# Recurrence gates of a hybrid encoder layer: one mixed contraction tile for both neighbours, put together by DMAs inside SBUF

## What is computed

```python
D_RNN = 1280; N_LRU_BLOCKS = 16; LRU_BLOCK = 80; LRU_C = 8.0
def rg_lru_branch(u, conv_w, conv_b, w_rg, b_rg, w_ig, b_ig, lru_lambda):
    u = depthwise causal convolution of width 4 over u, + conv_b
    ub = u.reshape(B, S, N_LRU_BLOCKS, LRU_BLOCK)
    r = sigmoid(einsum("bsnc,ncd->bsnd", ub, w_rg) + b_rg)
    i = sigmoid(einsum("bsnc,ncd->bsnd", ub, w_ig) + b_ig)
    log_a = -LRU_C * r * softplus(-lru_lambda)
    a = exp(log_a)
    b = sqrt(-expm1(2.0 * log_a)) * (i * u)
    _, h = lax.associative_scan(_lru_combine, (a, b), axis=1)   # h = a * h_before + b
    return h
...
h = rms_norm(x); proj = h @ w_in      # -> lru_u, lru_y, q, k, v, two merge gates
lru_out = rg_lru_branch(lru_u, ...) * gelu(lru_y)
attn_out = sliding window attention with sinks (q, k, v)
merged = g_lru * (lru_out @ w_lru_br) + g_attn * (attn_out @ w_attn_br)
x = x + rms_norm(merged @ w_out);  x = x + rms_norm(SwiGLU(rms_norm(x)))
```

## Time and profile before

| | us |
|---|---|
| median of three runs | 1734.54 |
| profiled execution, its own time | 1732.49 |
| its span | 1730.7 |
| PE busy / DVE / ACT / POOL | 1692.4 / 801.4 / 561.0 / 1320.2 |
| mean granted TensorE clock | 0.991 |
| gate matmuls (L424 to L426 on uc_hi, uc_lo) | 3 x 108 |

### The profile page before, as it was taken

The page is one execution under the profiler, slowest core; times in us unless marked ns, Lnnn a source line. Parts: engine busy times, 40 slices in busy tenths (PEclk is TensorE's granted clock), DMA queues, the critical chain, the costliest instruction groups (busy, mean ns, idle before and its releaser), DMA issues.

```text
span 1730.7 us, 26755 instructions
## 1 busy us (share of the span) xinstructions
PE 1692.4 (98%) x7676; PEld 1392.5 (80%) x7676; DVE 801.4 (46%) x878; ACT 561.0 (32%) x1034; POOL 1320.2 (76%) x1344
## 2 busy tenths in 40 slices
PE   8999999999999999999999999999999999999995
PEld 6787888888888878888888888888888888888884
DVE  5899736651277987766421733211611232111013
ACT  4577435442236765254422322111200211111000
POOL 5799966777788999777777877776777777666774
PEclk8999999999999999999999999999999999999997
DMA  4333332232343333422323434322433343224331
GB/s 142 102 88 89 116 98 85 79 98 94 108 128 106 90 89 108 155 75 76 96 94 103 140 130 143 109 96 93 137 100 95 111 143 132 94 95 141 96 97 60
DMA packets 111228, 183.15 MB, mean 106 GB/s; under 512 B 12352, under 2 KB 38208, under 8 KB 111168
## 3 DMA queue, kind: packets, MB, share of 16 engines
q1 hardware_dynamic: 97056, 156.15, 29.2%
q10 hardware_dynamic: 14112, 26.22, 4.5%
HBM read 173.94 MB, written 8.39 MB: 105 GB/s over the span
## 4 chain that ended last, share of the span: by engine, by line
PE 86%; issue 5%; POOL 4%; DVE 3%; ACT 1%; DMA 0%; POOLq 0%; ACTq 0%; SPq 0%; DVEq 0%
PE ps L426 27%; PE ps L425 26%; PE ps L424 26%; POOL w_hi L358 3%; POOL w_lo L361 1%; PE ps L486 1%; PE ps L565 1%; PE ps L487 1%; PE ps L488 1%; PE ps L555 0%; PE ps L557 0%; PE ps L556 0%; PE ps L580 0%; PE ps L579 0%; DVE rows L1482 0%
## 5 line engine op out<-in xcount | busy, mean ns | idle before, releaser
L361 POOL TENSOR_TENSOR w_lo<-w_raw,w_hi 128x512 fp32r<-128x512 f32 (+2 forms) x664 | 849.4, 1279 | 55.4
L358 POOL TENSOR_SCALAR w_hi<-w_raw 128x512 fp32r<-128x512 f32 (+2 forms) x664 | 466.5, 703 | 334.2 <-PE ps L426 261.1
L424 PE MATMUL ps<-h_hi,w_hi 128*128 128x512 f32 x1376 | 538.1, 391 | 9.9 <-POOL w_lo L361 7.5
L426 PE MATMUL ps<-h_hi,w_lo 128*128 128x512 f32 x1376 | 541.0, 393 | 0.0
L425 PE MATMUL ps<-h_lo,w_hi 128*128 128x512 f32 x1376 | 538.8, 392 | 0.0
L424 PEld LDWEIGHTS ps<-h_hi,w_hi 128*128 128x128 f32 x1376 | 258.4, 188 | 71.2 <-issue 6.4
L425 PEld LDWEIGHTS ps<-h_lo,w_hi 128*128 128x128 f32 x1376 | 258.4, 188 | 57.3
L426 PEld LDWEIGHTS ps<-h_hi,w_lo 128*128 128x128 f32 x1376 | 258.6, 188 | 54.3
L1122 DVE TENSOR_TENSOR acc<-acc,sq 128x512 f32<-128x512 f32 x55 | 66.3, 1206 | 226.7 <-ACT sq L969 201.7
L1447 DVE TENSOR_TENSOR tmp<-ps,tmp 128x512 f32<-128x512 f32 x44 | 30.4, 691 | 301.8 <-PE ps L426 301.8
L426 PE MATMUL ps<-f_hi,w_lo 128*128 128x512 f32 x352 | 138.7, 394 | 0.0
(11 more groups left out here) (193 smaller groups left out, 2431.3 us busy)
## 6 DMA issues: line engine op xcount, KB each, us to landing
w_raw<-w_f SPq DMA_DIRECT2D x176, 256.0 KB, 3.0
w_raw<-w_step SPq DMA_DIRECT2D x64, 256.0 KB, 2.6
w_raw<-w_b SPq DMA_DIRECT2D x64, 256.0 KB, 3.0
w_raw<-w_d SPq DMA_DIRECT2D x64, 256.0 KB, 2.7
w_raw<-w_a SPq DMA_DIRECT2D x96, 128.0 KB, 2.0
xs<-x_t ACTq DMA_DIRECT2D x32, 256.0 KB, 3.4
w_raw<-w_q SPq DMA_DIRECT2D x32, 256.0 KB, 3.2
w_raw<-w_o SPq DMA_DIRECT2D x32, 256.0 KB, 3.0
```

The costliest lines, as they stand in the source:

```text
L358: nc.gpsimd.tensor_scalar(w_hi[:, s, w], w_raw[:, s, w], 1.0, 0.0, ALU.mult, ALU.add).then_inc(w_hi_made, 1)
L361: nc.gpsimd.tensor_tensor(w_lo[:, s, w], w_raw[:, s, w], rd(w_hi[:, s, w]), ALU.subtract).then_inc(w_lo_made, 1)
L424: mm(out, w_hi[:, s, w], x_hi, start=(k == 0), stop=False)
L426: last = mm(out, w_lo[:, s, w], x_hi, start=False, stop=(k == total - 1))
```

## The change

For the six tiles with two neighbours (`MIXED` = 1, 2, 3, 6, 7, 8), the rows of the neighbours on which the gates depend lie in the upper half of tile j-1 (partitions 64 to 127) and in the lower half of tile j+1 (partitions 0 to 63). The change gathers these two halves in one tile, `mix_hi` and `mix_lo`, three buffers of each, in the memory of `v_hl`. ACT issues the gathering: in a new function `mix(h, j)`, called between `decay` and `gelu`, it copies partitions 0 to 63 of tile j into the mixed tile for j-1, and partitions 64 to 127 into the one for j+1, each as two DMAs (hi and lo). So tiles 2 and 7 issue four DMAs, the other tiles two each: 24 in each half. PE waits for the mixed tile's semaphore (all four DMAs) ahead of the gates of a mixed tile, and every gate has then 2 contraction tiles (tile 5 leaves out its zero one): 20 a gate, 40 in each half.

SP loads the weights of the gates in the same form: for a mixed block two DMAs of 64 partitions bring the neighbours' weight rows into one tile, a third brings the tile's own. POOL splits 256 columns in place of 384 and waits for two semaphores. In both streams the step and tail parts are written out in place of the loop. The weights in DRAM are unchanged.

```diff
+MIXED = (1, 2, 3, 6, 7, 8)
+GATED = {"step": 0, "tail": 8}
...
+        mix_hi = at("mix_hi", [P, 3, T], F32R, reg_v + 4 * KV_HEADS * 2 * HD)
+        mix_lo = at("mix_lo", [P, 3, T], F32R, reg_v + 4 * (KV_HEADS * 2 * HD + 3 * T))
...
+            def load_gates(dram, g, sizes, n, i0):
...
+                    wait_pos(sp_eng, w_lo_made, n + b - RING + 1)
...
+                    elif i in MIXED:
+                        sp_eng.dma_start(w_raw[0:P // 2, s, P:2 * P],
+                                         dram[g, 0:P // 2, off + 2 * P:off + 3 * P]).then_inc(mix_loaded[s], 16)
+                        sp_eng.dma_start(w_raw[P // 2:P, s, P:2 * P],
+                                         dram[g, P // 2:P, off:off + P]).then_inc(mix_loaded[s], 16)
+                        sp_eng.dma_start(w_raw[:, s, 0:P], dram[g, :, off + P:off + 2 * P])\
+                            .then_inc(w_loaded[s], 16)
...
+            def split_gates(sizes, n, i0):
...
+                    s, w = b % RING, slice(0, (4 if size == 4 else 2) * P)
...
+                        pool.wait_ge(mix_loaded[s], 32 * used[s])
...
+            def gates(h, j, n, slot):
+                J = j + KR * h
+                pe.wait_ge(uc_lo_made, J + (1 if j == KR - 1 else 2))
...
+                if j in MIXED:
+                    pe.wait_ge(mix_made[j % 3], 64 * (2 * h + 1 + (j > 5)))
+                tiles = [(j + d) % 4 for d in ((0, 1) if j in (0, 5) else (-1, 0))]
                 for g in range(2):
-                    project(4 + g, n + g, slot + g, [size], uc_hi, uc_lo, tiles=tiles)
+                    s, out = (slot + g) % RING, ps[:, 4 + g, :]
+                    pe.wait_ge(w_lo_made, n + g + 1)
+                    for k in range(2):
...
+                        mm(out, w_hi[:, s, w], x_hi, start=(k == 0), stop=False)
+                        mm(out, w_hi[:, s, w], x_lo, start=False, stop=False)
+                        last = mm(out, w_lo[:, s, w], x_hi, start=False, stop=(k == 1))
...
+            def mix(h, j):
+                if j + 1 in MIXED or j - 1 in MIXED:
+                    act.wait_ge(uc_lo_made, j + KR * h + 1)
+                for to, r in ((j - 1, slice(0, P // 2)), (j + 1, slice(P // 2, P))):
+                    if to in MIXED:
+                        act.dma_start(rd(mix_hi[r, to % 3, :]), rd(uc_hi[r, j % 4, :])).then_inc(mix_made[to % 3], 16)
+                        act.dma_start(rd(mix_lo[r, to % 3, :]), rd(uc_lo[r, j % 4, :])).then_inc(mix_made[to % 3], 16)
...
                     gate_root(h, j - 2)
                     decay(h, j - 2)
+                    mix(h, j)
                     gelu(h, j, n + 6, j % 4)
```

More of the change, by code:

```diff
@@ L214, in build @@
         w_loaded = [sem(f"w_loaded{i}") for i in range(RING)]
+        mix_loaded = [sem(f"mix_loaded{i}") for i in range(RING)]
+        mix_made = [sem(f"mix_made{i}") for i in range(3)]
         par_loaded = sem("par_loaded")
@@ L316, in load @@
                     off += size * P
+            def load_gates(dram, g, sizes, n, i0):
+                off, i, half = 0, i0, slice(0, P // 2)
+                for b, size in enumerate(sizes):
+                    s = b % RING
+                    wait_pos(sp_eng, w_lo_made, n + b - RING + 1)
+                    if size == 4:
+                        sp_eng.dma_start(w_raw[:, s, 0:CAP], dram[g, :, off:off + CAP])\
+                            .then_inc(w_loaded[s], 16)
[5 more added lines that the diff above has]
+                        sp_eng.dma_start(w_raw[:, s, 0:P], dram[g, :, off + P:off + 2 * P])\
+                            .then_inc(w_loaded[s], 16)
+                    else:
+                        at0 = off + (size - 2) * P
+                        sp_eng.dma_start(w_raw[:, s, 0:2 * P], dram[g, :, at0:at0 + 2 * P])\
+                            .then_inc(w_loaded[s], 16)
+                    off += size * P
+                    i += size < 4 and sizes[b - 1] < 4
             def stream(stages, bases):
@@ L323, in stream @@
                     first = 1 if base == 0 else 0
+                    if name in GATED:
+                        for g in range(groups):
+                            load_gates(dram, g, sizes, base + g * len(sizes), GATED[name] + 4 * g)
+                        continue
                     if first:
@@ L369, in stream @@
                     first = 1 if base == 0 else 0
+                    if name in GATED:
+                        for g in range(groups):
+                            split_gates(sizes, base + g * len(sizes), GATED[name] + 4 * g)
+                        continue
                     assert base % RING == 0 and len(sizes2) % RING == 0
@@ L500, in recurrent @@
                     project(0, n, slot, UNIT, h_hi, h_lo)
[L501 to L505, removed]
+                    gates(h, j - 2, n + 2, slot + 2)
                     wait_pos(pe, gelu_made, j + KR * h)
```

32 lines of the change are left out of this document (25 added, 7 removed).

## The result

The changed kernel takes 1739.07 us (median of ten runs, 1736.87 to 1742.36), the kernel before 1734.45 us in ten runs on the same chip (1731.69 to 1736.47). The ratio is 1.003, 95% interval 1.002 to 1.004: 0.3% slower, where 0.1% faster had been forecast. The time lies inside the predicted range, on the wrong side of the forecast.

The account below looks back on a forecast made before the run. It took the ACT loop, with gates waiting for copies behind decay, to set the pace: +1.85 us first half, -3.4 second, -1.6 in sum, 1734.54 to 1732.9 us. Range 1726.5 to 1740.

Parts of the forecast that it names:

- POOL's term: Gate blocks of 256 instead of 384 columns save POOL 0.76 us a step, 4.6 us a half over six steps.
- the loop on ACT: Step from gates through tanh, exp, root, DVE and decay back to gates; D(0) to D(7) forecast at 101.8 us.
- POOL as the bound: Rival: POOL stays the bound, mixed wait hidden, late start made up; 4.6 us a half, 1725.4 us, chance 0.13.
- The mixed step: Steps whose gates wait for copies issued behind decay: 5.5 us to the tanh plus 9.1 to decay, 14.6 us.
- The issue: Copies on ACT's queue behind D(i-1): 0.05 us to the first issue, 0.35 to the second, an issue taking 0.33.
- The landing: Copies inside SBUF: 2.0 us to land, as stores on the same queue, range 1.6 to 3.0.
- From tanh to decay: Part of a mixed step from the gate's tanh to its decay: 9.1 us, with POOL having less to do.
- The unmixed step: Two of seven steps (gates 4 and 5) have no mixed tile and keep the loop at 14.4 us.
- the clock falls more often: Rival: half clock also in the second half's G(1) or in G(6); 2.7 or 5.4 us, 1735.6 to 1738.3, chance 0.14.
- the late landing: Rival: copies land at 3.0 us, mixed steps take 15.2; 4.0 us a half, 8.0 in all, 1740.9, chance 0.18.
- The head: Tile 1's copies ahead of its gelu on ACT make D(0) 1.55 us late in each half, bounds 0.7 and 2.
- What was put at nothing: Steps' issues under decay (upper bound 0.3 us a step), SP's extra issues and the written-out streams (0 to 2 us): 0.

Follow-up runs that it names:

- nothing is paid: Changed kernel without copies; mixed gates contract over the left neighbour's tile, output not the reference's: 1720.71 us, ratio 0.9926 to the kernel before.
- where no gate waits: Changed kernel, copies issued but gates of a mixed tile not waiting for them: 1729.11 us; with the head's copies also moved behind the gelu: 1725.33 us.
- the early copies: Changed kernel with the steps' copies issued between root and decay instead of behind decay, head's copies unmoved: 1720.91 us, ratio 0.9929 to the kernel before.
- filling: Changed kernel with 6 to 16 unused matmuls on PE ahead of the wait before G(1), G(3) and G(6): 1735.30 us, ratio 1.0012 to the kernel before.
- POOL alone: Changed kernel without copies, POOL splitting 256 columns but PE still doing three contraction tiles: 1723.79 us, ratio 0.9947 to the kernel before.

## Why the prediction was wrong, step by step

**What bounds the kernel.** That PE's 86% of the chain would not turn into 19.2 us was right: 12.8 us come when nothing is paid. The forecast worked out POOL's term but did not put it in the sum, which went by the loop on ACT; POOL as the bound was a rival. With no copy in the way POOL is the higher limit (15.88 us a step with 384 columns, 14.95 with 256, against PE's 15.1 with 66 matmuls), and its 0.76 us a step was sized right. The sum also took it that what moves the tanh of gate 8 moves the end; from there to Q(2) the change saves 1.1 and 1.25 us, which it had left out.

**The mixed step.** The mechanism was right: gates behind the copies, copies behind decay, tanh behind the gates, and the stage's end with the tanh of gate 8. What failed is the price of the wait: 5.5 us from D(i-1) to the tanh of gate i, the same for every mixed gate. The trace has 6.1 at its best (87.17 to 93.31 for D(1) and gate 2), 6.7 and 6.8 for gate 8, and 7.5 to 9.9 for gates 1, 3 and 6. With all that follows from it the wait costs 9.5 us of the kernel. The terms:

- *The issue.* 0.05 and 0.35 with 0.33 an issue, from the loads of the earlier trace rows. Measured 0.47 and 0.61: the lo copy leaves at +0.51 and its issue ends at +1.12.
- *The landing.* 2.0 with a range of 1.6 to 3.0, its lower end from a saving by half the bytes for which no row was given. Measured 2.3 for hi and 2.8 for lo in the median, never under 2.2, and up to 4.6, above the range. By the Trainium skill (DMA: Bandwidth & Descriptors, Anatomy of one DMA), whose fit for DMAs issued by GpSimd has a term for the bytes as well, 128 KB would be an estimated 2.3 us. These copies are issued by ACT. The row of hi agrees with the estimate all the same; the lo copy right behind it does not. The prediction had named only the fixed part and left open that an SBUF target would answer sooner, which these rows don't show.
- *From tanh to decay* 9.1 were put down; it is 8.2 (78.95 to 87.17) and 8.4 (93.31 to 101.68). This was too high by about as much as the other two were too low in an undisturbed step. So the 14.6 of a mixed step was met (14.51) by two errors that cancel, which is luck. The unmixed step of 14.4 came as forecast (14.26 and 14.51).

**The steps that were not ordinary.** Between D(0) and D(7) the trace has 107.7 us in the first half and 110.8 in the second, where 104.5 (with one fall of the clock) and 101.8 were forecast; before it was 103.4 and 106.0. All of the miss between these two decays lies in six steps: those behind G(1), G(3) and G(6). There the gates start 3.9 to 5.2 us after decay, or the clock is at half, or both. The forecast had one fall of the clock, in G(1) of the first half, which came, with the start at 73.35 in place of 71.9; it made G(1) 2.3 us longer, where 2.7 were put down. It came four more times: G(6) in the first half and G(1), G(3) and G(6) in the second. That was the rival called "the clock falls more often", with a chance of 0.14 and a price of 2.7 or 5.4 us, 1735.6 to 1738.3. The other rival that points this way is the late landing, 1740.9. The measured 1739.1 lies between them, and both came together, which no case of the prediction allowed for, since each was worked out with the other at its likeliest value. The landing rival's own slope, 8 us for 1 us of landing, gives 1739.3 with the median of 2.8; that is chance, since it made every mixed step longer by 0.6, while the undisturbed ones stayed at 14.51 and the loss sat in three gates a half and in ACT's issues.

**The head.** 1.55 us a half were put down. The gelu of tile 1 starts 3.15 us later than in the earlier trace rows (46.43 to 49.58). Of this 1.1 lie ahead of the first copy: the stage starts that much later in this trace (`uc_hi` of tile 0 at 36.41, before at 35.30). The other 2.0 are the copies of tile 1. So D(0), 2.2 us later than in the earlier trace rows, is 1.1 us later by the head in the first half, less than put down, and in the second half 1.6 (28.29 against 26.73 us from `uc_hi` of tile 0), as put down. Against the same kernel with the head's copies moved it is 1.2 and 2.8, so something else in the change gives 1.2 back in the second half. The runs that load and split as the change does and have no copies ahead of the head's gelu take 25.5 us there, the one that only leaves matmuls out on PE 26.7. By the ratios the head's copies cost 4.9 us in both halves, or 3.3 where no gate waits, and 3.1 were in the sum: within what the ratios leave open, the term was right.

**What was put at nothing.** The copies' issues in the steps were called free under decay, "upper bound 0.3 us a step". They are not free: 5.2 us in sixteen steps, 0.3 a step, the upper bound. Two issues hold ACT by 0.52 us ahead of the gelu, four by 1.85. Part of it is seen in the step of tile 7; how the rest reaches the end was not followed further. SP's two more issues a block show no wait of POOL for a gate's load in the trace of the changed kernel. What the written-out streams cost was not measured apart; it lies within the 12.8 us.

**The signs in the profile.** Right: 84 matmuls less, POOL below 95%, half clock in G(1), the gates behind decay, steps of 14.4 to 14.7 where nothing disturbs (14.3 to 14.5). Wrong: 2.5 us from decay to gates (3.0 to 5.2), and the tanh of gate 8 (184.64 and 668.66, not 179.4 and 652.5). The gelu of tile 1 (49.58, not 48.0) and `conv_in` of tile 2 (60.23, not 59.5) came late, mostly with the start of the stage.

**The account by ratios.** 12.8 us gained by fewer tiles; 8.5 lost by issuing the copies where they stand (3.3 head, 5.2 steps); 9.5 lost by waiting for them, some 3.1 or more of it by the clock. That is +5.2 in sum, 0.3%. These differences add up by their making; what confirms them are the two kernels that undo a cause alone in the changed kernel: the head moved gives 4.9 back, and the early copies give 17.5 of the 18.0, though the head's copies stand where they stood. The prediction's -1.6 us had the loss at one wait of 5.5 us a step and one fall of the clock, and the issues in the steps at nothing; these are the steps of it that failed.

**Still open.** Why some landings take over 4 us where most take 2.3 to 2.8: no run was made for it. In the 3 us behind decay the DMA engines of the changed kernel are busy for 0.73 to 0.79 ahead of the late G(3) and G(6) of both halves, with SP's weight loads issued up to and across the copies, and for 0.58 to 0.62 ahead of G(2) and G(7), which start after 3.0 us. So loads at the same time are a likely cause, not a shown one, and G(8), after 3.5 and 3.7 us with the engines at 0.54, does not fit. How much of the wait is the clock: filling gave back 3.1 us, with two falls left, and in the one trace five pairs of gates were 9.1 to 9.5 us longer; nothing here narrows it further.

## What to carry to other kernels

Issue a DMA that feeds the next matmuls where its source is ready and the issuing engine would wait anyway, not behind the last instruction of the step: exchanging two lines made 0.3% slower into 0.7% faster. Where three engines are close to full, ask for each what it alone would give back: here the chain of one execution gave POOL 4%, and POOL alone gave 9.2 of 12.8 us. And where a new wait is priced, price the late case and what the idle engine loses together, for here they came together.

## What was not expected of the hardware

Two copies of 128 KB inside SBUF, issued one behind the other on ACT's queue, took 0.47 and 0.61 us to issue and 2.3 and 2.8 us to land in the median, with single ones at 4.3 and 4.6; one copy of 256 KB took 0.60 and 3.5. Inside SBUF they were not quicker than stores of 256 KB to DRAM, 2.0 to land, nor quicker to issue than loads of 256 KB, 0.33.

A wait of 2.40 us on PE was followed by half clock in one place (G(3) of the second half), while G(3) of the first half, after 1.93 us, kept the upper level, as PE did before the change after 2.49 us at Q(2). With the head's copies moved, half clock followed waits of 2.01 and 2.20 us (G(3) and G(7) of the first half, 0.63 over 103 to 107 and 0.57 over 165 to 169), and 2.65 us at G(6) between them did not bring it (1.00 over 149 to 153). So the length of the last wait alone did not tell.
